# Modulation weights loaded by columns, three first tiles begun on half the blocks, and a filling product in 23 attention items

## The reference

```
u = rms_norm(x, ln1) * (1 + scale1) + shift1
proj = u @ w_in
```

## Time and profile before

| | |
|---|---|
| median of 3 runs | 2228.36 us (2225.49 to 2229.49) |
| profiled execution | 2229.08 us, its span 2227.3 us |
| TensorE busy | 2194.3 us (99% of the span) |
| VectorE, ScalarE, GpSimd busy | 1297.0 us (58%), 858.4 us (39%), 25.2 us (1%) |
| mean granted TensorE clock | 0.992 of full speed |

### The profile page before, as it was taken

The page is one execution under the profiler, slowest core; times in us unless marked ns, Lnnn a source line. Parts: engine busy times, 40 slices in busy tenths (PEclk is TensorE's granted clock), DMA queues, the critical chain, the costliest instruction groups (busy, mean ns, idle before and its releaser), DMA issues.

```text
span 2227.3 us, 28694 instructions
## 1 busy us (share of the span) xinstructions
PE 2194.3 (99%) x10942; PEld 1833.7 (82%) x10942; DVE 1297.0 (58%) x1831; ACT 858.4 (39%) x1223; POOL 25.2 (1%) x24
## 2 busy tenths in 40 slices
PE   7999999999999999999999999999999999999998
PEld 5888888888888898888888888889878678888887
DVE  5677777767673475434475344354777756434344
ACT  5655555543222342322343222234455444222224
POOL 0000000000000000000000000000001000000000
PEclk8999999999999999999999999999999899999999
DMA  7423323324543334233223322223121002233321
GB/s 254 134 80 106 98 95 104 102 76 157 183 151 103 104 116 132 95 95 97 93 93 101 108 94 95 95 95 93 44 74 39 20 32 83 95 97 99 107 85 67
DMA packets 208141, 222.10 MB, mean 100 GB/s; under 512 B 9413, under 2 KB 200330, under 8 KB 205994
## 3 DMA queue, kind: packets, MB, share of 16 engines
q1 hardware_dynamic: 206362, 210.26, 29.2%
q10 hardware_dynamic: 1680, 10.49, 1.2%
HBM read 218.57 MB, written 2.16 MB: 99 GB/s over the span
## 4 chain that ended last, share of the span: by engine, by line
PE 93%; DVE 3%; DMA 2%; issue 1%; ACT 1%; ACTq 0%; DVEq 0%; SPq 0%
PE G L560 25%; PE G L562 25%; PE G L561 25%; PE G L611 2%; PE G L613 2%; PE G L612 2%; PE G L1065 1%; PE X L778 1%; PE X L1082 1%; DMA araw<-in_w_ada 1%; PE G L574 1%; PE G L576 1%; PE G L575 1%; PE X L1072 1%; PE X L1048 1%
## 5 line engine op out<-in xcount | busy, mean ns | idle before, releaser
L560 PE MATMUL G<-ahi,whi 128*128 128x512 f32 x1472 | 584.6, 397 | 0.0
L562 PE MATMUL G<-ahi,wlo 128*128 128x512 f32 x1472 | 574.5, 390 | 0.0
L561 PE MATMUL G<-alo,whi 128*128 128x512 f32 x1472 | 574.2, 390 | 0.0
L1891 DVE TENSOR_TENSOR wlo<-raw,whi 128x2048 fp32r<-128x2048 f32 (+3 forms) x172 | 386.9, 2249 | 240.8 <-ACT whi L1223 237.8
L1223 ACT ACTIVATE whi<-raw 128x2048 fp32r<-128x2048 f32 (+3 forms) x176 | 330.1, 1876 | 443.0 <-PE G L562 423.5
L560 PEld LDWEIGHTS G<-ahi,whi 128*128 128x128 f32 x1472 | 277.4, 188 | 58.1 <-issue 2.1
L562 PEld LDWEIGHTS G<-ahi,wlo 128*128 128x128 f32 x1472 | 277.0, 188 | 58.4
L561 PEld LDWEIGHTS G<-alo,whi 128*128 128x128 f32 x1472 | 277.3, 188 | 57.8 <-issue 1.9
L560 PE MATMUL G<-hhi,whi 128*128 128x512 f32 x784 | 305.9, 390 | 0.5 <-issue 0.5
L562 PE MATMUL G<-hhi,wlo 128*128 128x512 f32 x784 | 305.1, 389 | 0.0
L561 PE MATMUL G<-hlo,whi 128*128 128x512 f32 x784 | 305.1, 389 | 0.0
(11 more groups left out here) (428 smaller groups left out, 2865.8 us busy)
## 6 DMA issues: line engine op xcount, KB each, us to landing
raw<-in_w_in SPq DMA_DIRECT2D x43, 1024.0 KB, 5.1
raw<-in_w_up SPq DMA_DIRECT2D x38, 1024.0 KB, 5.3
raw<-in_w_down SPq DMA_DIRECT2D x32, 1024.0 KB, 5.1
raw<-in_w_gate SPq DMA_DIRECT2D x22, 1024.0 KB, 5.1
braw<-in_w_ada SPq DMA_DIRECT2D x12, 1024.0 KB, 5.2
raw<-in_w_in SPq DMA_DIRECT2D x20, 512.0 KB, 4.4
araw<-in_w_ada ACTq DMA_DIRECT2D x8, 1024.0 KB, 18.0
bc<-acum_dram SPq DMA_DIRECT2D x8, 1024.0 KB, 6.9
```

What stands on the lines that cost most here:

```text
L560: pe.matmul(bank[:], wh[:, j, f], rh[:, j, :], start=(j == 0), stop=False)
L561: pe.matmul(bank[:], wh[:, j, f], rl[:, j, :], start=False, stop=False)
L562: last = pe.matmul(bank[:], wl[:, j, f], rh[:, j, :], start=False, stop=(j == k - 1))
L1891: tt(wlo[s][:, 0:n], raw[s][:, 0:n], r32(whi[s][:, 0:n]), ALU.subtract).then_inc(lo_split, 1)
```

## The change

*Loads.* ACT's queue loads w_ada by columns: scale1 as four pieces of two row blocks (`ascale`), the first half of shift1 as two pieces, the X unit of group 0 (before, on SP's queue), and the second half of shift1 as three pieces (`ashift`). SP loads ln1, ln2 and b_ada under a semaphore of their own, then the dt weights, then the other vectors.

*Sums.* The first two row blocks of scale1 are multiplied by TensorE itself, 128 columns wide, with a column of silu(c) repeated. VectorE adds up the other six, then the two halves of shift1 one after the other. The sums over partitions have 128 columns of ones instead of one. Only columns that are later overwritten or read matter; the rest is unread.

*Activations.* ScalarE scales all four blocks of xs, makes `xc = coef * turned xs` straight from PSUM, then `ahi = xc + shift`. VectorE makes `alo` from xc, shift and ahi in one instruction. Blocks 0 to 3 come first; between their low parts VectorE adds up the second half of shift1, and blocks 4 to 7 follow. `OWN` is gone. An early dummy loads ScalarE's Sqrt table ahead of the squares.

*Low parts.* GpSimd clears pacc earlier and makes the low parts of the dt weights and of the X unit.

*First tiles.* TensorE goes over blocks 0 to 3 with the dt tile and both X tiles, then sums, turns the vectors, and does blocks 4 to 7 with the dt tile and the first X tile, then the second X tile, with `turn_dt` in it, now four transposes.

*Attention.* For items 26 to 40 and 45 to 52, `turn_p` issues one product of ones with the identity into its bank before the wait for the probabilities; nothing reads it.

```diff
+FILL_FIRST, FILL_SECOND = 2, 1
+FILLED = (*range(26, 41), *range(45, 53))
...
-        ahi, alo, xin, *araw = phase(*split_a, ("xin", [P, TB, D]), *((f"araw{u}", [P, UNIT]) for u in range(8)),
-                                     ("adacc", [P, UNIT]))
-        adacc = araw.pop()
-        xn = [araw[k // 4][:, k % 4 * T:(k % 4 + 1) * T] for k in range(KB)]
+        ahi, alo, xin, ascale, ashift, adacc = phase(*split_a, ("xin", [P, TB, D]), ("ascale", [P, KB, D]),
+                                                     ("ashift", [P, 2, KB, D // 2]), ("adacc", [P, UNIT]))
+        xc = [ascale[:, k // 2, k % 2 * T:(k % 2 + 1) * T] for k in range(KB)]
...
-            vec(v2[0:8, :], rows(a["ln1"][0]))
-            vec(v2[8:16, :], rows(a["ln2"][0]))
-            vec(v2[16:64, :], rows(a["b_ada"][0]))
+            sp.dma_start(v2[0:8, :], rows(a["ln1"][0])).then_inc(early_landed, 16)
+            sp.dma_start(v2[8:16, :], rows(a["ln2"][0])).then_inc(early_landed, 16)
+            sp.dma_start(v2[16:64, :], rows(a["b_ada"][0])).then_inc(early_landed, 16)
+            load(w_in[:, :, C_DT:C_DT + HEADS], n=HEADS)
...
+            loaded_by_act()
+            sp.wait_ge(first_landed[8], 16)
+            scan_turn(0, True, False, False, True)
...
+            for k in range(4):
                 turn_features(k, xin).then_inc(tile_done, 1)
+            mod = take_x(3)
+            pe.wait_ge(gone, 1)
+            pe.wait_ge(c_ready, 1)
+            pe.wait_ge(first_landed[0], 16)
+            for f in range(KB):
+                for k in range(2):
+                    last = pe.matmul(mod[:, f:f + P], ascale[:, k, f * P:(f + 1) * P],
+                                     cact[:, k:k + 1].broadcast_to([P, P]), start=(k == 0), stop=(k == 1))
+            last.then_inc(direct_done, 1)
+            pe.wait_ge(early_landed, 16 * EARLY_VECS)
+            pe.transpose(take_x(1)[:, 0:64], v2[0:64, :], ident[0:64, 0:64]).then_inc(aux_done, 1)
+            for k in range(4, KB):
+                turn_features(k, xin).then_inc(tile_done, 1)
             pe.wait_ge(scaled, TB)
+            for k in range(4):
                 turn_features(k, xs).then_inc(xn_done, 1)
+            def sums_by_ones(at, columns, used):
+                t["ada"].add()
+                pe.wait_ge(ada_acc, t["ada"].now())
+                for j, f in enumerate(columns):
+                    last = pe.matmul(mod[:, at + j:at + j + P], adacc[:, f * P:(f + 1) * P], ones[:],
+                                     start=True, stop=True)
+                    if j >= len(columns) - used:
+                        last.then_inc(ada_used, 1)
+            sums_by_ones(KB, range(KB, KB + 4), 2)
+            sums_by_ones(KB + 4, range(KB + 4, 2 * KB), 2)
+            turn_features(4, xs, take_g(1)).then_inc(xn_done, 1)
+            for k in range(5, KB):
+                turn_features(k, xs, take_x(k - 5)).then_inc(xn_done, 1)
+            sums_by_ones(2 * KB, range(4), 2)
...
+            def first_tiles(turn_dt):
                 s = next_unit()
                 bank, wd = take_g(2 * s), unit(whi[s], KB, 2 * HEADS)
+                sx = slot[0]
+                slot[0] ^= 1
+                t["n"].add()
+                banks, wh, wl = [take_g(2 * sx), take_g(2 * sx + 1)], unit(whi[sx]), unit(wlo[sx])
+                keep_clock(FILL_FIRST, banks[0])
+                def steps(j):
+                    high, low, dst = wd[:, j, :], wd[:, j, 0:HEADS], bank[0:HEADS, :]
...
+                def products(m, j):
+                    f = slice(m * P, (m + 1) * P)
...
+                for j in range(4):
+                    if j % 2 == 0:
+                        pe.wait_ge(first_low, j // 2 + 1)
+                    pe.wait_ge(act_ready, t["op"].now(j + 1))
+                    steps(j)
+                    for m in range(2):
+                        products(m, j)
+                sums_by_ones(2 * KB + 4, range(4, KB), 2)
+                turn_vectors()
+                pe.wait_ge(x_free[2], 1)
+                keep_clock(FILL_SECOND, X[2])
+                pe.wait_ge(lo_split, t["n"].now())
+                for j in range(4, KB):
+                    pe.wait_ge(act_ready, t["op"].now(j + 1))
+                    steps(j)
+                    products(0, j)
+                for j in range(4, KB):
+                    if j == 6:
+                        turn_dt()
+                    products(1, j)
...
-                    for half in range(2):
-                        last = pe.matmul(bank[:, c * HEADS:(c + 1) * HEADS], ss[0:2 * HEADS, c * P:(c + 1) * P],
-                                         ident[0:2 * HEADS, half * HEADS:(half + 1) * HEADS],
-                                         start=(half == 0), stop=(half == 1))
+                    last = pe.transpose(bank[:, 2 * c * HEADS:2 * (c + 1) * HEADS], ss[0:2 * HEADS, c * P:(c + 1) * P],
+                                        ident[0:2 * HEADS, 0:2 * HEADS])
...
+                if i in FILLED:
+                    pe.matmul(bank[:, 0:P], ones[:], ident[:], start=True, stop=True)
...
-            for u in range(8):
-                act.dma_start(araw[u][:], a["w_ada"][0][u * P:(u + 1) * P, 0:UNIT]).then_inc(first_landed[u], 16)
+            for u in range(4):
+                ks = slice(2 * u, 2 * u + 2)
+                act.dma_start(ascale[:, ks, :], w_ada[:, ks, D:2 * D]).then_inc(first_landed[u], 16)
+            for u in range(2):
+                ks = slice(4 * u, 4 * u + 4)
+                act.dma_start(ashift[:, 0, ks, :], w_ada[:, ks, 0:D // 2]).then_inc(first_landed[4 + u], 16)
+            act.dma_start(unit(raw[1]), w_in[:, :, C_X:C_X + GW]).then_inc(landed[1], 16)
+            for u, ks in enumerate((slice(0, 4), slice(4, 6), slice(6, 8))):
+                act.dma_start(ashift[:, 1, ks, :], w_ada[:, ks, D // 2:D]).then_inc(first_landed[6 + u], 16)
...
+            act.activation(warm[:], epsT[:], ACT.Sqrt)
...
-            for b in range(2):
+            for b in range(TB):
                 act.activation(xs[:, b, :], xin[:, b, :], ACT.Identity, scale=s4[:, b:b + 1]).then_inc(scaled, 1)
...
+            def scaled_block(k, bank, free):
+                act.wait_ge(xn_done, k + 1)
+                act.activation(xc[k], bank[:], ACT.Identity, scale=coef[:, k:k + 1]).then_inc(free, 1)
+            def shifted(half):
+                act.wait_ge(shift_ready, half + 1)
+                for k in range(4 * half, 4 * half + 4):
+                    act.activation(ahi[:, k, :], xc[k], ACT.Identity, bias=modT[:, 0, k:k + 1]).then_inc(val_hi, 1)
+            act.wait_ge(coef_ready, 1)
+            for k in range(4):
+                scaled_block(k, G[k], g_free[k])
             act.wait_ge(landed[1], 16)
             act.activation(whi[1][:, 0:UNIT // 2], raw[1][:, 0:UNIT // 2], ACT.Copy).then_inc(first_hi, 1)
             act.activation(whi[1][:, UNIT // 2:UNIT], raw[1][:, UNIT // 2:UNIT], ACT.Copy).then_inc(hi_split, 1)
+            for k in range(4):
+                act.wait_ge(g_free[k], 3)
+            shifted(0)
+            scaled_block(4, G[1], g_free[1])
+            for k in range(5, KB):
+                scaled_block(k, X[k - 5], x_free[k - 5])
+            act.wait_ge(g_free[1], 4)
+            for b, n in enumerate((2, 2, 1)):
+                act.wait_ge(x_free[b], n)
+            shifted(1)
...
+            pool.wait_ge(x_ready, KB)
+            pool.wait_ge(scaled, TB)
+            pool.memset(pacc[:], 0.0).then_inc(gone, 1)
+            pool.wait_ge(hi_split, 1)
+            both = unit(whi[0], KB, 2 * HEADS)
+            pool.tensor_tensor(both[:, :, HEADS:2 * HEADS], unit(raw[0], KB, HEADS), r32(both[:, :, 0:HEADS]),
+                               ALU.subtract).then_inc(lo_split, 1)
+            for c in range(4):
+                if c % 2 == 0:
+                    pool.wait_ge(*((hi_split, 2) if c else (first_hi, 1)))
+                cut = slice(c * T, (c + 1) * T)
+                pool.tensor_tensor(wlo[1][:, cut], raw[1][:, cut], r32(whi[1][:, cut]), ALU.subtract)\
+                    .then_inc(first_low if c < 3 else lo_split, 1)
...
+            def weighted(dst, src, k, first=False):
+                c = cact[:, k:k + 1]
+                return ts(dst, src, c, None, ALU.mult) if first else stt(dst, src, c, dst, ALU.mult, ALU.add)
+            scale_acc, shift_acc = adacc[:, D:2 * D], [adacc[:, h * T:(h + 1) * T] for h in range(2)]
+            dve.wait_ge(first_landed[1], 16)
+            for k in (2, 3):
+                link(weighted(scale_acc, ascale[:, k, :], k, k == 2))
+            token_factors()
+            dve.wait_ge(first_landed[2], 16)
+            for k in (4, 5):
+                link(weighted(scale_acc, ascale[:, k, :], k))
+            dve.wait_ge(first_landed[3], 16)
+            link(weighted(scale_acc, ascale[:, 6, :], 6))
+            link(dve.tensor_copy(v2T[:, 0:64], X[1][:, 0:64]))
+            dve.sem_inc(x_free[1], 1)
+            dve.wait_ge(direct_done, 1)
```

(48 more changed lines are left out.)

146 lines of the change are left out of this document (33 added, 113 removed).

## The result

The changed kernel takes 2250.29 us (median of 4, 2250.11 to 2250.48) where the kernel before takes 2228.65 on the same chip: ratio 1.0101, 95% interval 1.0089 to 1.0114. The forecast was 2224.6. The profiled execution has a span of 2248.6 us, 21.3 more than before.

The account below looks back on a forecast made before the run. TensorE, busy 99% of the span, bounds the kernel: time falls only through earlier dense work, regained clock or less waiting. Head 1.0 + attention 2.8 = 3.8 us gained, median 2228.36 to 2224.6, own range 2221.5 to 2227.

Parts of the forecast that it names:

- It issues eleven transfers instead of nine; eight took 4.34 us, so +1.1.: Head, ScalarE: two more DMA issues cost 1.1 us; first copy of xT starts at 14.7 instead of 15.27.
- 69.4: End of the head: TensorE goes on with the Z unit at 69.4 us instead of 70.41, 1.0 gained.
- DMA landings: Head: scale pairs land near 12.0, 14.9, 17.9, 20.8 us, first shift half 24.1 and 26.9, X weights 30.0.
- GpSimd over VectorE, "I take 0.8": Head: GpSimd's X lows, near 32 to 37 us, hold VectorE up by 0.8 us, one wait.
- the bound 2.75: Head: upper bound in us if every remaining piece of GpSimd's X lows holds VectorE once.
- Rival 2: GpSimd and VectorE exclude each other: head 1.7 us lost, attention 2.8 gained, 2227.3 us; chance 0.12.
- The sums over partitions, 2.25 or 1.1 more: Head: TensorE's scale sums take 2.25 us, 1.1 more at low clock; coef at 27.7 to 28.8.
- The dt tile's end, 50.7: Head: dt tile done at 50.7 us against 51.4; 49.3 to 50.3 by VectorE's undisturbed rows.
- Blocks, the chain behind the dt tile, the waits for B/C and Z: Head: an alo every 2.1 to 2.5 us, then waits of 1.3 for B/C and 2.8 for Z.
- the low clock behind the 2.3 us wait for Z: Sign of wrong: clock falls in the new waits near 54 and 67 us, each product after costing 0.2 more.
- Attention, net 2.8: Attention: fills holding the clock gain 4.4 us and cost 1.6, net 2.8 us gained.
- Rival 4: Attention: fills stand in the path, 5.8 us lost against the head's 1.0, 2233.2 us; chance 0.13.

Follow-up runs that it names:

- e4: The kernel before, its eight 1 MB modulation-weight transfers cut to four blocks by 512 columns each (2 KB rows, 4,096 packets instead of 1,024): 2238.14 us.
- e5: The kernel before, its eight 1 MB modulation-weight transfers cut to two blocks by 1024 columns each (4 KB rows, 2,048 packets instead of 1,024): 2231.30 us.
- e1: The changed kernel with the shift pieces and X weights issued by SP, after its vectors and once the second scale piece landed: 2232.97 us, ratio 1.0028.
- e7: The changed kernel with the shift pieces and X weights issued by SP at once, ahead of its vectors, without waiting: 2227.75 us, ratio 1.0006.
- e8: The changed kernel with GpSimd's four low pieces of the X weights cut from 512 columns to 8: 2245.43 us, ratio 1.0077.
- e3: The kernel before with only the unread products of the 23 attention items added: 2227.54 us, ratio 1.0003.
- e11: As e10, with TensorE's four sums of the second shift half moved ahead of block 3's products: 2230.25 us, ratio 1.0021.
- e13: As e7, with the low part of the X weights made by VectorE in two halves instead of by GpSimd: 2227.10 us, ratio 1.0002.
- e18: The kernel of e14 measured once more, unchanged: 2226.00 us, ratio 0.9996.
- e10: As e7, with three VectorE sums of the second shift half moved ahead of block 0's low: 2231.28 us, ratio 1.0020.
- e14: As e13, with one second-half sum ahead of block 0's low and TensorE's sums ahead of block 3's products: 2227.73 us, ratio 1.0001.

## Why the prediction was wrong

- *"It issues eleven transfers instead of nine; eight took 4.34 us, so +1.1."* **This step failed**: issuing ended at 25.9, not at 6.7. The price was taken per transfer; the rows of the transfers were known to shrink from 8 KB to 4, 2 and 1, and this was charged to the landing only. What the runs showed in its place: the issuing engine stands still while many packets of its queue are outstanding (e4 and e5 by the row length alone, e1 and e7 by the queue). It makes 19.1 of the 21.3 us by which the Z unit missed its 69.4.
- *DMA landings*: right. In e7 VectorE could begin on the second, third and fourth scale piece at 14.4, 17.0 and 20.3 (forecast 14.9, 17.9, 20.8); in the changed kernel the data lay ready.
- *GpSimd over VectorE, "I take 0.8"*: mis-sized, 2.3 (e8); inside the bound 2.75. The prediction used half of what the GPSIMD Engine Reference of the Trainium skill (section 1, Specifications) states: the page also names VectorE instructions in a two-port mode. The trace agrees: the one-input TENSOR_SCALAR was hit hardest, 0.48 to 1.51. Rival 2 had the mechanism right, though not its price in all: with the issuing undone the head is level, not 1.7 worse.
- *The sums over partitions, 2.25 or 1.1 more*: 19 us earlier coef would have come at 28.8, the upper end, at half clock; in e7 27.5.
- *The dt tile's end, 50.7*: 1.0 early. ScalarE copies it at 72.03 in the changed kernel (less the 19.1 that is 52.9) and at 51.73 in e7. Both lie behind the 49.3 to 50.3 of VectorE's undisturbed rows; the contention above is the difference.
- *Blocks, the chain behind the dt tile, the waits for B/C and Z*: right. From the second on, lows every 2.24 us, waits of 1.14 and 2.32 (forecast 1.3 and 2.8), 90.66 − 77.17 = 13.5 from B/C to Z. With ScalarE free and nothing else changed the head is 70.35 (e7): level with before, where 1.0 less was forecast. What was named as a sign but not priced is the low clock behind the 2.3 us wait for Z, 3.2 us long, 1.6 to 1.8 us lost up to the first logits, there in the changed kernel and e1 and not in e7.
- *Attention, net 2.8*: mis-sized as a single value. The clock came back as forecast, 3.4 us of half clock instead of 16, but the time from the first logits to the end fell by 0.8 only, and the medians of all runs show nothing that can be told. Executions whose clock stayed up did gain 2.5 to 3.2 there (e3, e11, e13, e18), so the mechanism is there; what failed is that one product an item would hold the clock every time. That the fills' own cost takes the rest of the gain is argued, not measured apart.

Rival 4, the one on the slower side, had the fills in the path; none had an engine held up by its own issuing.

## What to carry to other kernels

Price a DMA issue by the packets it makes (rows times blocks), not by the call, and add up what its queue still holds: an engine that also computes should not hand over a series of short-row transfers ahead of its first work; give them to an engine with nothing behind them. Idle time beside GpSimd's work is not free time for VectorE: move GpSimd's work first (e10 and e11 against e14, part of the difference being the clock). A fill for the clock is proved only over many executions.
